# Value tiles of both branches computed ahead of the heads by a seven-product scheme

## What is computed

```python
h = _rms(x, norm_g)                      # 512 tokens x 2048
u = h @ w_in                             # 2048 x 13312
(hq, hi, hf_fwd, hf_bwd, hgate, nq, nk, nv, ngate, m_a, m_b) = split(u)
oa = _hgrn2_bidir(hq, hi, hf_fwd, hf_bwd, ...)      # 8 heads of 128, v = hi
ya = (_rms(oa) * silu(hgate)) @ w_branch_a
ob = _neighbourhood_attention(_rms(nq), _rms(nk), nv, rpb)   # 8 heads of 128
yb = (ob * silu(ngate)) @ w_branch_b
y = sigmoid(m_a) * ya + sigmoid(m_b) * yb
x = x + y @ w_out
x = x + (p @ w_ple) * sigmoid(_rms(x) @ w_ple_gate)
```

## Time and profile before

| | us |
|---|---|
| median of 3 runs | 1839.7 (1839.49 to 1839.81) |
| the profiled execution | 1839.31 |
| its span | 1837.6 |
| one head of the loop (542.16 to 657.19) | 115.0 |
| eight heads, from 316.87 to about 1232 | 915 |

### The profile page before, as it was taken

How to read it: one execution, slowest core, us unless ns; L and a number is a source line. 1 busy time by engine, 2 the same in 40 slices (tenths; PEclk the granted TensorE clock), 3 DMA queues, 4 the chain that set the end, 5 groups by cost and what they waited for, 6 DMA issues and landing times.

```text
span 1837.6 us, 25708 instructions
## 1 busy us (share of the span) xinstructions
PE 1813.3 (99%) x9521; PEld 1559.0 (85%) x9521; DVE 1113.9 (61%) x1324; ACT 830.3 (45%) x1137; POOL 202.6 (11%) x205
## 2 busy tenths in 40 slices
PE   6999999999999999999999999999999999999998
PEld 5899999888888888888888888888888888888887
DVE  6977777575866758667586675864544422245332
ACT  7444444555736557365573655734322232234221
POOL 4000000220402204022040220400000000010000
PEclk9999999999999999999999999999999999999999
DMA  7243453423323233232332323334555534465332
GB/s 227 91 131 115 127 156 96 129 71 98 96 77 101 76 97 93 78 98 79 97 92 80 97 80 97 91 109 143 160 144 143 176 122 164 166 235 188 121 127 74
DMA packets 291909, 217.80 MB, mean 119 GB/s; under 512 B 8826, under 2 KB 254617, under 8 KB 290321
## 3 DMA queue, kind: packets, MB, share of 16 engines
q1 hardware_dynamic: 288384, 205.04, 36.6%
q0 software_dynamic: 3472, 12.05, 1.9%
HBM read 192.45 MB, written 24.61 MB: 118 GB/s over the span
## 4 chain that ended last, share of the span: by engine, by line
PE 96%; DVE 2%; ACT 1%; issue 1%; DMA 1%; SPq 0%; DVEq 0%; ACTq 0%
PE mm_ps L1649 16%; PE mm_ps L1647 16%; PE mm_ps L1648 16%; PE mm_ps L1859 5%; PE mm_ps L1858 5%; PE mm_ps L1860 5%; PE ax_ps L1634 2%; PE ax_ps L1635 2%; PE ax_ps L1636 2%; PE ax_ps L1649 2%; PE ax_ps L1647 2%; PE ax_ps L1648 2%; PE ax_ps L1859 2%; PE ax_ps L1858 2%; PE ax_ps L1860 2%; PE mm_ps L1636 2%
## 5 line engine op out<-in xcount | busy, mean ns | idle before, releaser
L330 DVE TENSOR_TENSOR w_lo<-w_raw,w_hi 128x1024 fp32r<-128x1024 f32 (+1 forms) x232 | 316.3, 1364 | 499.1 <-ACT w_hi L321 497.2
L321 ACT ACTIVATE w_hi<-w_raw 128x1024 fp32r<-128x1024 f32 (+1 forms) x232 | 262.2, 1130 | 650.9 <-PE mm_ps L1649 350.2
L1647 PE MATMUL mm_ps<-act_hl,w_hi 128*128 128x512 f32 x1216 | 485.6, 399 | 0.0
L1649 PE MATMUL mm_ps<-act_hl,w_lo 128*128 128x512 f32 x1216 | 474.6, 390 | 0.0
L1648 PE MATMUL mm_ps<-act_hl,w_hi 128*128 128x512 f32 x1216 | 474.0, 390 | 0.0
L1649 PEld LDWEIGHTS mm_ps<-act_hl,w_lo 128*128 128x128 f32 x1216 | 228.2, 188 | 49.0
L1648 PEld LDWEIGHTS mm_ps<-act_hl,w_hi 128*128 128x128 f32 x1216 | 228.7, 188 | 45.0
L1647 PEld LDWEIGHTS mm_ps<-act_hl,w_hi 128*128 128x128 f32 x1216 | 228.6, 188 | 44.5
L812 ACT ACTIVATE q_hi<-q_raw 128x1024 fp32r<-128x1024 f32 x84 | 87.5, 1057 | 141.7 <-DVE q_raw L1162 81.2
L1858 PE MATMUL mm_ps<-w_hi,act_hl 128*128 128x512 f32 x384 | 149.9, 390 | 0.0
L1860 PE MATMUL mm_ps<-w_lo,act_hl 128*128 128x512 f32 x384 | 149.4, 389 | 0.0
(11 more groups left out here) (270 smaller groups left out, 3219.0 us busy)
## 6 DMA issues: line engine op xcount, KB each, us to landing
w_raw<-in_w_in SPq DMA_DIRECT2D x152, 512.0 KB, 3.7
q_raw<-in_w_in SPq DMA_DIRECT2D x56, 512.0 KB, 5.6
w_raw<-in_w_ple_gate SPq DMA_DIRECT2D x20, 768.0 KB, 4.2
w_raw<-in_w_out SPq DMA_DIRECT2D x16, 768.0 KB, 4.2
w_raw<-in_w_branch_a SPq DMA_DIRECT2D x16, 512.0 KB, 3.8
w_raw<-in_w_branch_b SPq DMA_DIRECT2D x16, 512.0 KB, 3.8
g_ab<-gate_dram SPq DMA_DIRECT2D x14, 512.0 KB, 4.3
gate_dram<-c_out SPq DMA_DIRECT2D x12, 512.0 KB, 5.0
```

The source lines that it names most:

```text
L321: nc.scalar.activation(w_hi[:, s, 0:width], w_raw[:, s, 0:width], ACT.Copy).then_inc(hi_done, 1)
L330: nc.vector.tensor_tensor(w_lo[:, s, 0:width], w_raw[:, s, 0:width], w_hi[:, s, 0:width].bitcast(F32), ALU.subtract).then_inc(lo_done, 1)
L1647: MM(bank, wh, m_hi[:, k0 + k, :], start=start and k == 0, stop=False)
L1649: mm = MM(bank, wl, m_hi[:, k0 + k, :], start=False, stop=stop and k == kn - 1)
```

## The change

The tiles HI and NV leave the heads. A new stage stands between the blocks and the heads: for `hi` and then for `nv` (`GROUPS = 2`) the full product of 512 tokens x 2048 with 2048 x 1024 is computed by the seven-product scheme in 28 units. Here the activations are the stationary operand and the weights move, 512 columns wide, so the result has the tokens in the partitions and needs no transpose. A unit is 12 matmuls; its slab (two depth tiles x 512 columns, 512 KB) is split by ACT and DVE as before. 16 of the 28 units of a group need a difference of two slabs (`row_sum`), and the products are put together in 14 additions of 512 columns on DVE (`row_evict`) and 2 copies on ACT. The results go to DRAM (`store_rows`), and each head fetches its `val` (place 4 of SP's units) and its `n_v` (place 13).

A head has 14 units. The places stay 18: places 6, 7, 14 and 15 have no unit, and the other work stands at the places where it stood. All eight heads are written out, no loop is left there. SP's requests for `z_a`, `bias` and `z_b` follow other units than before.

```diff
-    NU = 18
+    TILES = [HQ, HF, HB, HG, NQ, NK, NG]
+    NJ, NU = len(TILES), 2 * len(TILES)
+    STEPS = 18
+    STEP_UNIT = {i: 2 * TILES.index(i // 2) + i % 2 for i in range(STEPS) if i // 2 in TILES}
+    GROUPS = 2
+    P_ALL = P_ROWS + 28 * GROUPS
...
+        def row_unit(j):
+            if j < 8:
+                return (0, 1)[j % 2], j // 2
+            if j < 16:
+                return (2, 3)[j % 2], (j - 8) // 2
+            if j < 24:
+                return (6, 5)[j % 2], (j - 16) // 2
+            return 4, j - 24
+        ROW_SUMS = {**{8 + n: n + 1 for n in range(8)}, **{17 + 2 * n: 9 + n for n in range(4)}, **{24 + n: 13 + n for n in range(4)}}
+        def row_hi(act, g, j):
+            num = P_ROWS + 28 * g + j
+            if j in ROW_SUMS:
+                act.wait_ge(r_sum, 16 * g + ROW_SUMS[j])
+            else:
+                row_ready(act, g, j)
+            act.wait_ge(p_unit, num - 2)
+            nc.scalar.activation(q_hi[:, num % RING, :], r_in[:, row_slot(j), :], ACT.Copy).then_inc(qhi_done, 1)
...
@@ SP @@
+            def store_rows(g, n):
+                sp.wait_ge(r_evict, 14 * g + (2, 8, 12, 14)[n])
...
+            def bring_v(h):
+                sp.wait_ge(o_done, h)
+                sp.dma_start(val[:, :].rearrange("p (t d) -> p t d", t=NT),
+                             val_dram[0].rearrange("(t p) n -> p t n", p=P)[:, :, h * P:(h + 1) * P]).then_inc(val_in, 16)
...
             def head(h):
+                us = Units(NU * h)
                 for i in range(NU):
...
+                    if i == 4:
+                        bring_v(h)
+                    if i == 13:
+                        if h:
+                            sp.wait_ge(pv_done, 4 * h)
+                        bring_windows(h)
@@ DVE @@
+            for g in range(GROUPS):
+                for j in range(28):
+                    row_lo(dve, g, j)
...
+                    for n, at in enumerate((11, 18, 19, 25, 26, 27)):
+                        if j == at:
+                            row_evict(g, n)
+                    if j + 1 in ROW_SUMS:
+                        row_sum(g, j + 1)
@@ PE @@
+            def row_group(g):
+                for j in range(28):
...
+                    pe.wait_ge(qlo_done, num + 1)
+                    for t in range(2):
+                        tok = slice(t * P, (t + 1) * P)
+                        for k in range(2):
+                            c = slice(k * 512, (k + 1) * 512)
+                            wh, wl = q_hi[:, num % RING, c], q_lo[:, num % RING, c]
+                            m = p_side(u, 2 * kp + k)
+                            o = row_bank(u, t)
+                            MM(o, m[:, 0, tok], wh, start=kp == 0 and k == 0, stop=False)
+                            MM(o, m[:, 1, tok], wh, start=False, stop=False)
+                            mm = MM(o, m[:, 0, tok], wl, start=False, stop=kp == 3 and k == 1)
+                    mm.then_inc(p_unit, 1)
...
-            def turn_v():
-            def turn_windows():
...
@@ every engine @@
             def head(h):
-                us = Units(0, NU, h)
-                for i in range(NU):
-                    split_lo(dve, us, i + AHEAD)
+                us = Units(NU * h)
+                for i in range(STEPS):
+                    if i in STEP_UNIT:
+                        split_lo(dve, us, STEP_UNIT[i] + AHEAD)
...
-            with dve.Fori(1, H) as h:
+            for h in range(1, H):
                 head(h)
```

More of the change, by code:

```diff
@@ L146, in build_kernel @@
             q_lo = sb("q_lo", [P, RING, 1024], F32R, where=pre)
+            with ExitStack() as rows_:
+                r_in = sb("r_in", [P, 8, 1024], where=rows_)
+                r_u = sb("r_u", [P, 2, 2, 512], where=rows_)
+                r_c = sb("r_c", [P, 2, 2, 512], where=rows_)
             q_raw = sb("q_raw", [P, 6, 1024], where=pre)
@@ L184, in build_kernel @@
             z_a = sb("z_a", [P, S], where=heads)
-            v_t = sb("v_t", [P, S], where=heads)
+            sb("spare", [P, S], where=heads)
             temp = sb("temp", [P, S], where=heads)
@@ L234, in build_kernel @@
         g_out_stored = [sem("g_out_stored0"), sem("g_out_stored1")]
+        r_ready = [sem(f"r_ready{n}") for n in range(8)]
+        r_sum, r_p1, r_evict = (sem(n) for n in ("r_sum", "r_p1", "r_evict"))
+        r_stored = [sem("r_stored0"), sem("r_stored1")]
+        val_in, nv_in = sem("val_in"), sem("nv_in")
         s_sum, s_hi_done, s_lo_done = (sem(n) for n in ("s_sum", "s_hi_done", "s_lo_done"))
@@ L456, in pre_stored @@
                 eng.wait_ge(c_stored[n], 16 * LOOPS)
+            for n in range(2):
+                eng.wait_ge(r_stored[n], 96)
         def branch_ps(slot, b):
@@ L707, in _ @@
             head(0)
-            with pool.Fori(1, H) as h:
+            for h in range(1, H):
                 head(h)
@@ L842, in _, with copy_p1 @@
                 pre_blocks(r)
+            def copy_p1(g):
+                act.wait_ge(p_unit, P_ROWS + 28 * g + 7)
+                if g == 0:
+                    act.wait_ge(c_stored[2], 16 * LOOPS)
+                    act.wait_ge(p_evict, 7 * len(BLOCKS))
+                else:
+                    act.wait_ge(r_evict, 14 * g)
+                for t in range(2):
+                    A(r_u[:, 0, t, :], row_bank(0, t), ACT.Copy).then_inc(r_p1, 1)
+            for g in range(GROUPS):
+                for j in range(28):
+                    row_hi(act, g, j)
+                    if g == 0 and j == 4:
+                        block_gate(LOOPS - 1, 2)
+                    if j == 10:
+                        copy_p1(g)
             for i in range(AHEAD):
                 split_hi(act, Units(0), i)
-            block_gate(LOOPS - 1, 2)
             def chain(h, d):
@@ L979, in _ @@
             head(0)
-            with act.Fori(1, H) as h:
+            for h in range(1, H):
                 head(h)
@@ new lines, in _ @@
+            for g in range(GROUPS):
+                for j in range(28):
+                    row_lo(dve, g, j)
+                    if g == 0 and j in (1, 2):
+                        evict(LOOPS - 1, 2, j + 4)
+                    if g and j == 2:
+                        row_evict(g - 1, 6)
+                    for n, at in enumerate((11, 18, 19, 25, 26, 27)):
[3 more added lines that the diff above has]
+                        row_sum(g, j + 1)
@@ L1382, in head @@
             def head(h):
-                us = Units(0, NU, h)
-                for i in range(NU):
-                    split_lo(dve, us, i + AHEAD)
-                    if not isinstance(h, int):
+                us = Units(NU * h)
+                for i in range(STEPS):
+                    if i in STEP_UNIT:
+                        split_lo(dve, us, STEP_UNIT[i] + AHEAD)
+                    if h > 0:
                         late(i, h - 1)
@@ new lines, in row_group @@
+            def row_group(g):
+                for j in range(28):
+                    u, kp = row_unit(j)
+                    if kp == 0 and g == 0:
+                        if u == 0:
+                            pe.wait_ge(p1_ready, len(BLOCKS))
+                        if u < 4:
+                            pe.wait_ge(p_evict, 7 * (len(BLOCKS) - 1) + (1, 5, 6, 7)[u])
+                    elif kp == 0 and u < 4:
+                        pe.wait_ge(r_evict, 14 * (g - 1) + (10, 8, 12, 14)[u])
+                    if kp == 0 and u >= 4:
+                        if u == 5:
+                            pe.wait_ge(r_p1, 2 * g + 2)
+                        else:
+                            pe.wait_ge(r_evict, 14 * g + {6: 2, 4: 4}[u])
+                    num = P_ROWS + 28 * g + j
+                    pe.wait_ge(qlo_done, num + 1)
+                    for t in range(2):
+                        tok = slice(t * P, (t + 1) * P)
[8 more added lines that the diff above has]
+                    mm.then_inc(p_unit, 1)
@@ L1769, in head @@
             def head(h):
-                us = Units(0, NU, h)
-                for i in range(NU):
-                    j = i // 2
-                    if i % 2 == 0:
-                        tile_free(h, j)
-                    columns(us, i, mm_ps[:, j % 3, :], 8 * (i % 2), 8, i % 2 == 0, i % 2 == 1, act_hi, act_lo)
-                    if not isinstance(h, int):
+                us = Units(NU * h)
+                for i in range(STEPS):
+                    if i in STEP_UNIT:
+                        u = STEP_UNIT[i]
+                        n = NJ * h + u // 2
+                        if u % 2 == 0:
+                            tile_free(n)
+                        columns(us, u, mm_ps[:, n % 3, :], 8 * (u % 2), 8, u % 2 == 0, u % 2 == 1, act_hi, act_lo)
+                    if h > 0:
                         late(i, h - 1)
@@ L1817, in _ @@
                 pre_blocks(r)
+            for g in range(GROUPS):
+                row_group(g)
             head(0)
-            with pe.Fori(1, H) as h:
+            for h in range(1, H):
```

285 lines of the change are left out of this document (192 added, 93 removed).

## The result

The change made the kernel slower by 4.0%: 1912.6 us (median of 4 runs, 1911.2 to 1913.8) after 1839.8, ratio 1.0396 with an interval of 1.0383 to 1.0409. The forecast was 1874.1, in a range of 1846 to 1900. The direction was right and the time was not: the kernel lost 72.9 us where 34.4 were forecast.

What follows compares the result with a forecast made beforehand. PE, busy 99% of the span, was taken to bound the kernel: 1839.3 - 182.9 (work leaving) + 152.5 (work added) + 20.3 (stage waits) + 44.5 (head waits) = 1873.7, stated as 1874.1 us, range 1846 to 1900.

Steps and rivals of the forecast that it cites:

- parts 1 and 2: PE's matmul work: 182.9 us leave the eight heads, 152.5 us come in the new stage at 0.227 us a matmul.
- the sum: Whole kernel: 1839.3 - 182.9 + 152.5 + 20.3 + 44.5 = 1873.7 us, given as 1874.1 against the median.
- rival (b): New stage and heads: no waits in either, 1809.3 us; chance 0.04.
- part 3: New stage: PE waits because DVE's difference and low half take 3.56 us against PE's 2.72 a unit; +20.3 us.
- Rival (d): New stage: weight slabs land late, at 7 us and more costing 15 to 25 us, 1895 us; chance 0.07.
- part 4: Heads: PE waits at place 6, places 8 to 11 and places 13 to 15, 5.5 us a head, +44.5 us together.
- rival (c): Heads, places 14 and 15: PE's clock falls after the waits, 22 to 43 us, say 1905; chance 0.07.
- the prediction's lower level there: After the first wait of 12.12 us: PE at 1.2 GHz, read from ten transposes at 0.24 us each.
- the reading of 1.4: Place 6 of a head: PE waits 1.4 us for ACT's copy `prob_t`, ready at 580.4.
- Rival (a): Heads: ACT and DVE keep PE's pace through places 5 to 14, so no waits there, 1829.6 us; chance 0.08.

Runs made afterwards that it cites:

- The last kernel: The 1821.0 us kernel (new stage and heads reordered, table load moved), plus last four loads of a group and their differences earlier: 1812.5 us, ratio 0.9852.
- the experiment alone: The changed kernel with unused matmuls added where PE waits, 10 at place 6, 12 and 5 at place 15: 1897.7 us after 1912.6.

## Why the prediction was right, and where it was wrong

**What leaves PE and what it gets (parts 1 and 2): right.** With its waits gone the stage takes 153.5 us, and a head 92.4, of which 0.3 are a wait for a low half; the sum had 152.5 and 92.1. The matmuls with moving weights cost the same 0.227 to 0.229 us from start to start. The last kernel is at 1812.5 where the sum without any wait was 1809.3, rival (b).

**Waits of the new stage (part 3): right in size and in cause.** 18.4 us above 152.5, forecast 20.3, and the row of difference, high half and low half that part 3 read from the blocks is what it was, 3.49 us for 3.56. Differences of units 8 to 15 made one unit further ahead took out half of it, 9.9 us. The rest went when loads were placed earlier and the last differences moved as well; that edit changed both at once, so their shares are not told apart. Rival (d), slabs that land late, had no part in the changed kernel: they land in 4.3 us in the median, and in the new stage no difference, high half or low half waits for one; DVE waits for `q_hi` there, 52.4 us over 45 times, and ACT for differences and for PE.

**Waits of the heads (part 4): the step that failed.** Its steps measure so, in the head from 689.54 on. Here a wait is counted from start to start, less what the matmul in front costs, which gives 0.1 to 0.2 us more than the idle time that the profile shows:

| | sum | measured |
|---|---|---|
| place 6, `prob_t` | 1.4 | 2.6 |
| slow clock behind it | 0 | 1.6 |
| places 8 to 11 | 0.1 | 0.4 |
| place 15, second mean | 2.8 | 2.9 |
| its states | 1.2 | 1.1 |
| slow clock behind them | 0 | 1.7 |
| matmuls | 92.1 | 92.1 |
| **head** | **97.6** | **102.4** |

The range left out what made it wrong: its upper end of 1900 has longer waits, but no slow work behind them. There are two mistakes, both of omission. First, the clock: part 4 put the work behind a wait at its full speed without a reason. The prediction had the slow clock as rival (c) with a chance of 0.07, priced at 22 to 43 us for places 14 and 15; it happened at places 6 and 15 in each of the seven later heads, and cost some 3.3 us of each, 15.0 us net in the experiment alone. The rows at hand had one wait of 12 us with slow work behind it and one of 1.2 without. (The granted clock of that stretch is shown as 1.00, so that the prediction's lower level there rests on the lengths alone; in the heads the clock column shows 0.50.) A head had waits in between these, and nothing in the rows said that they were harmless; the sum took them so. The rule that the prediction set against its own sum, in "TensorE: Matmul & The Clock Gate" of the Trainium skill, section "HAM oscillation — how this bites in real kernels", says that a PE with gaps between bursts falls back again and again. The trace agrees: clock 0.50 at 729.54 and again at 777.33.

Second, the prediction followed places 5 and 6 of ACT with the times of the loop's rows, 580.00 for `prob_t`, and costed the writing out of the heads at nothing. "The loop overhead that is gone never showed as a wait of PE" was true, and beside the point: what changed was on which instruction a wait stands. The difference was there to be read in the order of ACT's instructions in a head of the loop (first two lines) and of the changed kernel (last two):

```
L869 ACT_TABLE_LOAD
L869 ACTIVATE base_q<-dif 128x512 [waits dif_ready]
L1035 ACT_TABLE_LOAD [waits dif_ready]
L1035 ACTIVATE base_q<-dif 128x512 [waits intra_done]
```

It costs 19.2 us here (with the slow unit that it brings about), 10.4 where places are covered, and nothing in the kernel before. Without it the wait of place 6 is 1.1 us, so the reading of 1.4 was right for the loop's order of waits.

**Rival (a), the cover holds,** was argued against rightly for this order of units; but the reason given (a chain of four steps with no unit in front) names the remedy too. With the units spread out, the heads reached it.

**Still open:** the clock stayed up after one wait of 2.40 us and fell after another of 2.41 at the same place; what decides between them the runs do not tell. Of the 38.5 us of the miss, 3.0 remain in the kernel in which both causes are taken away. Its heads take 5.3 us more than the sum's: 0.5 in each of the later seven, which is the wait for `lev_q` at place 11 (0.6 us from start to start, 0.1 in the sum), and the rest in the first; the new stage gives back 1.9.

## What to carry to other kernels

Work that leaves the busiest engine also leaves the steps that were hidden behind it. List those steps with their lengths, and spread what remains so that one piece stands in front of each; here that was worth 72 us, about the 73 that the change had cost, and 82 with the table load moved. Cover at one place counts only if no later wait on the same row takes it back, and a stretch of slow clock counts only if no later wait absorbs it, so edit the last wait of the row first. When a loop is written out, look at which instruction each wait ends up on.

## What the hardware showed that was not expected

- At the lower clock matmuls of 512 columns started 0.427 us apart and those of 128 columns 0.213, for 0.227 and 0.111 at the upper: 1.9 times.
- The clock fell behind waits of 2.4 and 2.7 us in the heads, mostly but not always, once behind one of 2.1, and it did not behind one of 1.06. Matmuls that nothing uses kept it up where they filled the waits, and made the kernel 15 us faster.
- A table load of ACT (1.28 us) can be held back by the waits of the instruction that it serves: 2.15 us of idle time and then the load, where the load could have run in the idle time.
